# The projection of a hybrid decoder layer, two tiles at a time and in halves of 64 rows

## The reference, cut to what matters

```python
h = rms_norm(x, norm1_g[l])                      # x: (1, 512, 1024)
proj = h @ w_in[l]                               # w_in: (1024, 3072)
dq, dk, dv, rq, rk, rv, rg = jnp.split(proj, PROJ_SPLITS, axis=-1)
...
mix = jnp.concatenate([d_out.reshape(B, S, DIFF_WIDTH), r_out], axis=-1)
x = x + mix @ w_o[l]
h2 = rms_norm(x, norm2_g[l]).reshape(B * S, D)
x = x + moe(h2, ...).reshape(B, S, D)            # top 4 of 32 experts
out = rms_norm(x, norm_f_g)
```

## Time and profile before

| what | us |
|---|---|
| median of 3 runs (lowest, highest) | 1472.73 (1472.57, 1479.18) |
| profiled execution | 1473.39 |
| its span | 1471.7 |
| TensorE busy | 1441.0 (98%) |
| VectorE busy | 1277.7 (87%) |
| ScalarE busy | 1019.0 (69%) |
| L714, L715, L719, busy | 68.8, 68.5, 47.1 |
| ACT L1218 and DVE L1509, mean of one | 0.69, 0.75 |

### The profile page before, as it was taken

How to read it: one execution, slowest core, us unless ns; L and a number is a source line. 1 busy time by engine, 2 the same in 40 slices (tenths; PEclk the granted TensorE clock), 3 DMA queues, 4 the chain that set the end, 5 groups by cost and what they waited for, 6 DMA issues and landing times.

```text
span 1471.7 us, 21956 instructions
## 1 busy us (share of the span) xinstructions
PE 1441.0 (98%) x6833; PEld 1183.4 (80%) x6833; DVE 1277.7 (87%) x1120; ACT 1019.0 (69%) x876; POOL 240.9 (16%) x232
## 2 busy tenths in 40 slices
PE   7999899999999999999999999999999999999997
PEld 6888578778888888888888888888888888888885
DVE  5465747799999999999999999999999999999998
ACT  5423734667777777777777777777777777777774
POOL 0100302412111111111111111212111111111111
PEclk9999999999999999999999999999999999999999
DMA  9442101899999999999999999999999999999994
GB/s 342 177 182 120 44 0 66 303 345 373 365 371 357 375 363 370 367 364 379 364 376 371 379 368 358 389 369 363 373 372 368 370 367 372 367 375 365 367 358 168
DMA packets 131391, 471.72 MB, mean 321 GB/s; under 512 B 15304, under 2 KB 15596, under 8 KB 131176
## 3 DMA queue, kind: packets, MB, share of 16 engines
q1 hardware_dynamic: 118160, 451.46, 81.7%
q0 software_dynamic: 13024, 19.88, 5.5%
q10 hardware_dynamic: 184, 0.08, 0.0%
HBM read 467.44 MB, written 32.51 MB: 340 GB/s over the span
## 4 chain that ended last, share of the span: by engine, by line
PE 91%; DVE 4%; issue 2%; ACT 2%; DMA 1%; DVEq 0%; ACTq 0%
PE pair L993 24%; PE pair L985 24%; PE pair L987 24%; PE pair L714 3%; PE pair L719 3%; PE pair L715 3%; PE pair L999 2%; PE pair L1011 2%; PE pair L975 2%; DVE split L1815 1%; PE pair L856 1%; PE pair L871 1%; PE pair L858 1%; DMA ring<-in_w_moe_in 1%; ACT split L1325 0%
## 5 line engine op out<-in xcount | busy, mean ns | idle before, releaser
L1815 DVE TENSOR_TENSOR split<-ring,split 128x2048 fp32r<-128x2048 f32 x396 | 891.8, 2288 | 71.4 <-ACT split L1325 71.2
L1325 ACT CAST split<-ring 128x2048 fp32r<-128x2048 f32 x396 | 760.0, 1920 | 193.1 <-PE pair L993 190.7
L985 PE MATMUL pair<-split,operands 128*128 128x512 f32 x1584 | 630.0, 398 | 1.0 <-DVE operands L1821 1.0
L987 PE MATMUL pair<-split,operands 128*128 128x512 f32 x1584 | 618.0, 390 | 0.0
L993 PE MATMUL pair<-split,operands 128*128 128x512 f32 x1584 | 424.8, 390 | 0.9 <-DVE split L1815 0.9
L993 PEld LDWEIGHTS pair<-split,operands 128*128 128x128 f32 x1584 | 297.1, 188 | 65.1 <-DVE split L1815 2.1
L985 PEld LDWEIGHTS pair<-split,operands 128*128 128x128 f32 x1584 | 297.7, 188 | 60.1 <-DVE operands L1821 1.4
L987 PEld LDWEIGHTS pair<-split,operands 128*128 128x128 f32 x1584 | 297.9, 188 | 58.5
L2094 POOL DMA_INDIRECT expert_sums<-work,list_cur x32 | 61.8, 1932 | 455.3 <-PE pair L993 423.8
L2087 POOL DMA_INDIRECT work<-h_rows,token_next x34 | 75.2, 2211 | 183.4 <-DMA token_next<-slot_lists 166.7
L1334 ACT CAST operands<-pair 128x512 fp32r<-128x512 f32 x66 | 38.8, 589 | 68.8 <-PE pair L993 39.9
(11 more groups left out here) (268 smaller groups left out, 1149.4 us busy)
## 6 DMA issues: line engine op xcount, KB each, us to landing
ring<-in_w_moe_in SPq DMA_DIRECT2D x264, 1024.0 KB, 9.1
ring<-in_w_moe_out SPq DMA_DIRECT2D x132, 1024.0 KB, 9.9
ring<-in_w_in SPq DMA_DIRECT2D x12, 1024.0 KB, 10.5
ring<-in_w_o SPq DMA_DIRECT2D x4, 1024.0 KB, 10.3
resid<-in_x SPq DMA_DIRECT2D x4, 512.0 KB, 5.2
expert_sums<-zero_rows SPq DMA_DIRECT2D x4, 512.0 KB, 11.9
h_rows<-work SPq DMA_DIRECT2D x4, 512.0 KB
work<-expert_sums SPq DMA_DIRECT2D x4, 512.0 KB, 5.2
```

The lines of the kernel that those rows point to most:

```text
L985: pe.matmul(dst[:, f, :], left_hi[:, k0 + k, :], hi[c.buffer][:, k, cols], start=(start and k == 0), stop=False)
L987: pe.matmul(dst[:, f, :], left_lo[:, k0 + k, :], hi[c.buffer][:, k, cols], start=False, stop=False)
L1325: act.copy(hi[c.buffer], raw[c.slot]).then_inc(hi_made, 1)
L1815: dve.tensor_tensor(lo[c.buffer], raw[c.slot], hi[c.buffer].bitcast(F32), ALU.subtract).then_inc(lo_made, 1)
```

## The change

For chunks 1 to 10 the tiles are taken two at a time by a new helper. Of the twelve products of a tile and chunk, eleven are made as two matmuls of 64 rows each. In the first part of a call the upper rows of tile i and the lower rows of tile i + 1 (or the other way round, by swap) follow each other, into two banks. Then one product of each tile is made whole, with 128 rows, then the rows change tiles. A semaphore, one_way_done, is raised by the last half of the first part and waited for after the whole products. proj_ready rises by two per call, and both proj_by_act and proj_by_dve are waited for ahead of a call. Chunks 0 and 11 stay as they were.

```diff
-        sp_passed = sem("sp_passed")
+        one_way_done = sem("one_way_done")
...
+            def half_rows(r):
+                return slice(r * (P // 2), (r + 1) * (P // 2))
+
+            def two_tiles(i, c):
+                b, a, s = c // 2, c % 2, c % PARTS
+
+                def halves(swap, left, right, k, begin, end=False):
+                    for t in ((0, 1) if swap == 0 else (1, 0)):
+                        rows = half_rows(t ^ swap)
+                        mm = pe.matmul(bank[NT * (b % 2) + i + t], left[rows, KH * a + k, of_tile(i + t)], right[s][rows, k, :],
+                                       start=begin, stop=end)
+                    return mm
+
+                for k in range(KH):
+                    halves(a, hT_hi, w_hi, k, a == 0 and k == 0)
+                    halves(a, hT_lo, w_hi, k, False)
+                if i == 0:
+                    pe.wait_ge(w_lo_made, c + 1)
+                for k in range(KH - 1):
+                    mm = halves(a, hT_hi, w_lo, k, False)
+                mm.then_inc(one_way_done, 1)
+                for t in range(2):
+                    pe.matmul(bank[NT * (b % 2) + i + t], hT_hi[:, KH * a + KH - 1, of_tile(i + t)], w_lo[s][:, KH - 1, :],
+                              start=False, stop=False)
+                pe.wait_ge(one_way_done, 2 * (c - 1) + i // 2 + 1)
+                for k in range(KH - 1):
+                    halves(1 - a, hT_hi, w_lo, k, False)
+                for k in range(KH):
+                    halves(1 - a, hT_hi, w_hi, k, False)
+                    mm = halves(1 - a, hT_lo, w_hi, k, False, a == 1 and k == KH - 1)
+                return mm
...
-            for c in range(1, NCHUNK):
+            for c in range(1, NCHUNK - 1):
+                b, a = c // 2, c % 2
+                pe.wait_ge(w_hi_made, c + 1)
+                for i in range(0, NT, 2):
+                    if a == 0 and b >= 2:
+                        pe.wait_ge(proj_by_act, 2 * (b - 2) + i // 2 + 1)
+                        pe.wait_ge(proj_by_dve, 2 * (b - 2) + i // 2 + 1)
+                    mm = two_tiles(i, c)
+                    if a == 1:
+                        mm.then_inc(proj_ready, 2)
+                if a == 0:
+                    mm.then_inc(half_block_done, 1)
+
+            for c in range(NCHUNK - 1, NCHUNK):
```

## The result

The kernel is slower, by 0.5 to 0.7%. Beside each other the changed kernel took 1485.79 us in the median of 6 runs (1482.74 to 1488.72), the kernel before 1476.96 us of 6; the ratio is 1.0068, with an interval of 1.0045 to 1.0091. In a later comparison it was 1484.95 us against 1475.77, ratio 1.0049 (1.0030 to 1.0068). The ratios are not exactly those of the medians. The profiled execution was 1482.74 us with a span of 1481.1 us, 9.4 us over the span of before.

What follows compares the result with a forecast made beforehand. TensorE's stream was taken to bound the kernel. 42 switches at 0.198 us gave +8.3 us, all other terms 0, so the median goes from 1472.73 to 1481.0 us; range 1475 to 1486, the forecast's own 1479.9 to 1482.1.

Steps and rivals of the forecast that it cites:

- What bounds the kernel: TensorE, 98% busy and waiting for nothing from 26 to 136 us; a microsecond added in the projection lengthens the kernel equally.
- Do halves run side by side: In the projection's pairs, two halves on different rows and banks run at once and cost one whole product; 0 for concurrency.
- A pair's slot is 0.2267 us, cost 0: Each of 440 slots of paired halves takes as long as a whole product; lower end -5.9 us.
- A switch is 0.198 us: Each change of TensorE between 128 and 64 rows costs this, uncovered; 42 of them make 8.3 us.
- The reason for the switch's price: A change of mode drains TensorE: 0.09 us until the next load, then 0.11 us of loading with nothing beside it.
- The new wait, evictions, buffers: 0: The one_way_done wait is over before it is reached; 15 us of slack hide ScalarE's copy starting up to 2.7 us later.
- The additional instructions: 0: Issuing the projection's additional 440 loads and matmuls, four instructions per 0.227 us, costs nothing.
- halves out of step: Rival, 12%: the lower half runs 0.107 us behind, ending each of 40 one-way stretches later; +4.3 us, 1485.3 us.
- The reading of the row at 147.09 us: Last L719 before a switch, with no load beside it, takes 0.23 us, so halves keep the 0.0134 us.
- the shorter stream: Rival, 18%: halves lose the 0.0134 us beyond their columns, so the sum is +2.4 us, 1475.1 us.
- taking turns: Rival, 5%: one-pass halves writing two banks can't run at once; +100 us, about 1581 us.
- a cheap switch: Part of the not-slower rival, 5%: with the short stream, switches below 0.147 us; at most -5.9 us, 1466.8 us.

Runs made afterwards that it cites:

- all tiles one way: Changed kernel with all twelve products as halves, all four tiles of a chunk one way before any is turned; 1.0011 of the kernel before, stretch 109.05 us.
- with the wait: Changed kernel with all twelve products as halves, the turn made by waiting for the last half alone; 1.0089 of the kernel before.
- doubled switches: Changed kernel with each tile's first low product whole too, four changes of mode a call; 1.0142 of the kernel before, stretch 126.87 us.
- the kernel with whole products: Changed kernel's tiles by twos, proj_ready by twos and covered wait, but every product whole; 0.9999 of the kernel before, stretch 108.80 us.
- 256 columns: Kernel before with each product of chunks 1 to 10 as two matmuls of 256 columns; projection's values differ, only the stretch is read: 115.19 us.
- lone halves: Changed kernel without every half product of the lower rows, so not computing the layer; 1.0066 of the kernel before, stretch 118.52 us.
- the one with whole products and a wait: Tiles by twos with whole products, TensorE waiting for its own last product in the middle of each call; 1.0080 of the kernel before.

## Why the prediction was right or wrong

- **What bounds the kernel**: right. Nothing of the delay was absorbed before the experts; 10.0 us at the first scores, 9.4 at the end.
- **Do halves run side by side**: right, and shown by leaving half of them out. One sign failed: pairs were to start within 0.01 us of each other, and in the changed kernel they drift to 0.04 us apart before each whole product. In the kernels with all tiles one way and with the wait they stay within 0.004.
- **A pair's slot is 0.2267 us, cost 0**: right for the steady slot, wrong as a sum over 440 slots, and this is the step that failed. The term came to 20 x 0.07 = 1.4 us: after each return to halves the first slots are uneven, 0.03 us, and the lower halves end up 0.04 us late. I had rows for a part of it: L987 at 278.89 us is followed by steps of 0.23 us and more in the same kernel. I took the exposed load out of that place and didn't look at the next products. They would have given 0.03 us a restart, 0.6 us in all, so less than half. What makes the slots uneven stays open.
- **A switch is 0.198 us**: right. In the changed kernel 0.21 and 0.19, with doubled switches 0.209 with the uneven slots in it. 42 of them are 8.3 us, as summed.
- **The reason for the switch's price**: right in its parts (0.09 us with nothing streaming, then an exposed load), but the mode is only one way to get there; a wait for an own product costs 0.37 to 0.39 us.
- **The new wait, evictions, buffers: 0**: right, 0.00 us in the kernel with whole products. **The additional instructions: 0**: right, since the kernel with 960 halves is 0.25 us over, a switch of 0.20 and one settling.
- **The sum**: +8.3 us forecast, +9.4 us in the profile. In the stretch 117.1 us was forecast and 118.5 measured.
- **The absolute time**: 1481.0 us forecast, 1485.79 measured, outside the 1479.9 to 1482.1 that I gave the forecast. By the medians only 0.5 us of the 4.8 are the change (8.8 us measured, 8.3 forecast; by the profiles it is 1.1). The other 4.2 us are the base, the larger error: I took the median of three runs, 1472.73 us, for the kernel before, and it took 1476.96, 1476.16, 1474.97 and 1475.77 us in the medians of the later comparisons. The three runs shown had a spread of 6.6 us, almost as large as the forecast, and I centred the range on the lowest pair. That the measured time lies inside the whole range, 0.2 us under its end of 1486, is luck: that end was there for halves out of step (1485.3 us), which did not occur.
- **The reading of the row at 147.09 us**: it gave 0.23 against 0.21 us from starts with two decimals, and said that the 0.0134 us is the product's own. The slot was kept at 0.2267 us as forecast, but whose part it is was not settled (256 columns).
- **The rivals**: the shorter stream is refuted (lone halves at 0.2267 us, and 480 slots of halves at 0.2272); out of step by 0.107 us did not occur, since the halves are at most 0.04 us apart and 22 lone halves take as long as 44; taking turns did not occur; a cheap switch did not occur.

## What to carry to other kernels

Splitting a full contraction into halves of 64 rows wins nothing where whole products already hide their loads: two halves fill one slot. What it can cost is the change between 64 and 128 rows, 0.20 us each with nothing to cover it, and 0.03 to 0.07 us of uneven slots behind; count the changes, sort the work by mode, and look for places where they alternate already. When a rate is taken from the steady state, look also at the ten instructions after each restart, and when a base is taken from three runs that differ by as much as the change, put that spread into the range.

## What the runs showed of the hardware that I had not expected

Every one-pass product with its load takes 0.0133 us more than its columns, at 256 and at 512 of them. About ten slots after a restart are uneven, in lone halves and in whole products after a wait alike (0.06 us in sum).

And a source of the spread between runs. All kernels have a wait of 2.8 us in the first expert pass. In the kernel before's profile the clock stays full behind it; in the profile of the kernel with whole products by twos, whose projection is the same to the hundredth, it falls to the lower level, 1.2 GHz, for eight products, and their steps are 0.43 us in place of 0.23 (timeline, then busy time with the granted clock, 0.81, where the kernel before has 1.00):

```profile
298.31 0.50 PE L1027 MATMUL pair<-split,operands 128*128 128x512 f32 x1
298.61 0.63 PE L1029 MATMUL pair<-split,operands 128*128 128x512 f32 x1
299.04 0.63 PE L1027 MATMUL pair<-split,operands 128*128 128x512 f32 x1
...
294.00:303.00 9.00, 6.24 (x25) 4.73 (x24) 8.14 (x14) 2.54 (x3) 1.73 (x3) 0.81 0.95 349
```

Eight such steps are 1.6 us. The 20 runs of the kernel before in one comparison had mean granted clocks from 0.993 to 0.998 and times from 1470.59 us (at 0.998) to 1480.19 (at 0.993). Over a whole run 0.005 of the clock is about 7 us, most of that distance.

What stays open: the two kernels drained by waits and the one with doubled switches had 0.993 in the mean of their runs (4 to 6 each, the kernel before 0.996 beside them) and lost 3 to 5 us beyond their stretches. Their profiles show where the largest fall lies, long after the projection. These are 200 to 235 us in the kernel with halves and a wait, in the one with whole products and a wait, in the one with doubled switches, and in the kernel before:

```profile
200.00:235.00 35.00, 33.54 (x183) 26.54 (x180) 15.64 (x41) 8.22 (x42) 0.00 (x0) 0.85 0.00 1
...
200.00:235.00 35.00, 33.54 (x155) 26.26 (x152) 15.68 (x43) 7.79 (x40) 1.14 (x10) 0.85 0.00 0
...
200.00:235.00 35.00, 30.97 (x175) 24.74 (x175) 16.06 (x42) 11.73 (x43) 0.00 (x0) 0.80 0.00 1
...
200.00:235.00 35.00, 34.59 (x177) 28.07 (x176) 16.49 (x46) 11.34 (x36) 2.13 (x15) 1.00 0.04 16
```

All other profiles have 1.00 there. So the extra loss goes with a lower clock behind the projection and not with the restarts themselves. Why the clock falls there in these three, some 50 us after the last stop in the projection, no run settles; no profile shows a fall within the stretch.
